# First weight copies and gate-up products ahead of finding and picking in the entry to the expert loop

## The reference, cut to what matters

```python
def _swiglu(x, w_gu, w_down):
    g, up = jnp.split(x @ w_gu, 2, axis=-1)
    return (jax.nn.silu(g) * up) @ w_down

def _moe(u, router_w, router_b, exp_w_gu, exp_w_down, shared_w_gu, shared_w_down):
    scores = jax.nn.sigmoid((u @ router_w).astype(jnp.float32))
    _, idx = lax.top_k(scores + router_b.astype(jnp.float32), TOP_K)
    ...
    routed = lax.map(lambda a: _routed_experts(a[0], a[1], a[2], exp_w_gu, exp_w_down), (u, idx, wts))
    return routed + _swiglu(u, shared_w_gu, shared_w_down)
```

## Time and profile before

| | us |
|---|---|
| median of 3 runs | 1243.19 |
| lowest and highest of them | 1238.89, 1243.43 |
| the profiled execution's own time | 1243.38 |
| its span in the trace | 1241.7 |
| from find(0) to the loop's first gate_up(1), in the trace | 582.71 to 609.02 |
| one step of the loop | 11.86 |

### The profile page before, as it was taken

How to read it: one execution, slowest core, us unless ns; L and a number is a source line. 1 busy time by engine, 2 the same in 40 slices (tenths; PEclk the granted TensorE clock), 3 DMA queues, 4 the chain that set the end, 5 groups by cost and what they waited for, 6 DMA issues and landing times.

```text
span 1241.7 us, 20074 instructions
## 1 busy us (share of the span) xinstructions
PE 1198.1 (96%) x5713; PEld 705.4 (57%) x5714; DVE 753.3 (61%) x1283; ACT 464.4 (37%) x549; POOL 289.3 (23%) x323
## 2 busy tenths in 40 slices
PE   5899999999999999998999999999999999999995
PEld 5688887777888888883434344343443443434332
DVE  4532457586562676867556566565565656767568
ACT  5562223746422413231324334333343443444301
POOL 1000000000000000003344353443444435545400
PEclk9798999999999999999999999999999999999988
DMA  9633502353485485646788889888888898999596
GB/s 342 185 125 102 170 35 102 102 183 135 158 323 202 140 279 191 220 174 242 285 334 331 313 319 342 315 322 325 312 335 299 323 338 325 418 410 412 223 422 252
DMA packets 88593, 321.56 MB, mean 259 GB/s; under 512 B 13040, under 2 KB 16344, under 8 KB 66152
## 3 DMA queue, kind: packets, MB, share of 16 engines
q1 hardware_dynamic: 69192, 279.69, 61.2%
q0 software_dynamic: 14432, 32.85, 6.9%
q10 hardware_dynamic: 4928, 8.49, 2.0%
HBM read 292.35 MB, written 48.24 MB: 274 GB/s over the span
## 4 chain that ended last, share of the span: by engine, by line
PE 89%; DVE 6%; issue 2%; ACT 2%; DMA 1%; DVEq 0%; POOL 0%; SPq 0%; POOLq 0%; ACTq 0%
PE psum L1666 33%; PE psum L1900 28%; PE psum L1910 14%; PE psum L1889 4%; PE psum L1639 2%; PE psum L1768 1%; DVE stage L1602 1%; PE psum L1699 1%; PE psum L1939 1%; DMA ring<-in_ada_w 1%; PE psum L1757 1%; PE psum L1824 1%; PE psum L1728 1%; PE psum L1960 1%; PE psum L1680 1%
## 5 line engine op out<-in xcount | busy, mean ns | idle before, releaser
L1900 PE MATMUL psum<-w_now,xT 128*64 128x512 f32 x1568 | 347.3, 595 | 0.6 <-DVE w_now L1500 0.6
L1900 PEld LDWEIGHTS psum<-w_now,xT 128*64 128x64 f32 x1568 | 108.7, 137 | 197.4 <-issue 196.2
L733 POOL COPY w_now<-stage 128x2048 f32 x79 | 149.6, 1911 | 284.6 <-PE psum L1910 239.3
L1910 PE MATMUL psum<-w_now,mask 128*64 128x512 f32 x784 | 179.1, 599 | 4.0 <-POOL w_now L733 4.0
L1006 ACT ACTIVATE w_now<-stage 128x2048 f32 x79 | 147.6, 1906 | 37.6 <-issue 35.0
L468 DVE TENSOR_TENSOR w_lo<-ring,w_hi 128x1024 fp32r<-128x1024 f32 x80 | 94.6, 1222 | 84.2 <-ACT w_hi L461 82.3
L1666 PE MATMUL psum<-uT_hi,w_hi 128*128 128x512 f32 x352 | 139.0, 395 | 1.1 <-DVE w_lo L468 1.1
L1666 PE MATMUL psum<-uT_hi,w_lo 128*128 128x512 f32 x352 | 137.0, 389 | 0.0
L1666 PE MATMUL psum<-uT_lo,w_hi 128*128 128x512 f32 x352 | 137.0, 389 | 0.0
L461 ACT ACTIVATE w_hi<-ring 128x1024 fp32r<-128x1024 f32 x80 | 82.7, 1056 | 123.5 <-PE psum L1666 60.7
L1013 ACT ACTIVATE sel<-psum 128x256 f32<-128x256 f32 x49 | 18.9, 385 | 290.5 <-PE psum L1900 290.5
(11 more groups left out here) (357 smaller groups left out, 1674.2 us busy)
## 6 DMA issues: line engine op xcount, KB each, us to landing
stage<-in_exp_w_gu SPq DMA_DIRECT2D x106, 1024.0 KB
stage<-in_exp_w_down SPq DMA_DIRECT2D x53, 1024.0 KB
ring<-in_w_in SPq DMA_DIRECT2D x56, 512.0 KB, 5.4
expert_rows<-zero_fill SPq DMA_DIRECT2D x16, 1024.0 KB, 8.7
ring<-in_ada_w SPq DMA_DIRECT2D x32, 512.0 KB, 4.8
stage<-expert_rows SPq DMA_DIRECT2D x12, 1024.0 KB, 20.8
ring<-in_ada_w SPq DMA_DIRECT2D x4, 1024.0 KB, 13.4
scale_w<-in_ada_w SPq DMA_DIRECT2D x4, 1024.0 KB, 14.7
```

Of the source, the lines that this page charges most:

```text
L733: pool.tensor_copy(w_now[:, q, 4:6], staged(turns[q] + STAGES - 1, 4, 2)).then_inc(dn_moved, 1)
L1900: mm = pe.matmul(moe_bank(GU)[at, :], xT[:, s % 2, k, at], gu_part(q, k), start=(k == 0), stop=(k == KT - 1))
L1910: mm = pe.matmul(moe_bank(Y0 + g)[at, :], hT[:, j, at], dn_part(q, j, g), start=(j == 0), stop=(j == 1))
```

## The change

Four engines could be concerned; three programs are edited (ScalarE, VectorE, TensorE). No instruction is added or removed, only the order of each engine's own work changes.

```diff
@@ ScalarE
             act.nop().then_inc(y_ready, 2)
+            act.wait_ge(tables_ready, 1)
+            move_second(0)
             rows_turned(0, 0)
-            act.wait_ge(tables_ready, 1)
             shared_gate(1)
-            move_second(0)
+            silu(0)
             rows_turned(1, 1)
-            silu(0)
             move_second(1)
@@ VectorE
             find_rows(1, 1)
+            move_first(0)
             pick_rows(2)
             shared_up(0)
             find_rows(2, 2)
             pick_rows(3)
-            move_first(0)
             find_rows(3, 3)
             pick_rows(AHEAD)
+            gated_up(0)
             shared_up(1)
-            gated_up(0)
             move_first(1)
@@ TensorE
             find(1)
             shared_products(4)
-            find(2)
-            shared_products(1)
             wait_emptied(pe, "bstart_row")
             turn_rows(0, 0, 16)
             shared_products(2)
-            find(3)
-            shared_products(4)
-            turn_rows(1, 1, 16)
             pe.wait_ge(tables_ready, 1)
             wait_emptied(pe, ("sgu", 0))
             gate_up(0, 0, pe.value_load(copies_thru[0:1, 0:1], min_val=1, max_val=TABLE))
+            find(2)
+            shared_products(2)
+            find(3)
+            shared_products(3)
+            turn_rows(1, 1, 16)
```

## The result

The changed kernel takes 1249.03 us (median of 5 runs, 1248.67 to 1251.66), the kernel before 1243.19: a ratio of 1.0067 with a 95% interval of 1.0051 to 1.0082, so 6.3 to 10.2 us slower. I had forecast 1244.8, in a range up to 1248.5, and 0.90 for no change beyond half a per cent.

A forecast was written before the change was run, and what follows sets the result against it. TensorE was taken to bound the kernel. Its 2.0 us of idle would become 1.05 + 0.65 + 0.95 + 1.1 = 3.75, gate_up(1) 1.6 later, so 1243.19 goes to 1244.8 us, range 1240.5 to 1248.5.

The forecast's parts named there:

- The bound: Whole kernel: TensorE bounds it, busy for 1198.1 of 1241.7 us, with no other engine over 61%.
- the 2.0 us as all that there was to win: TensorE's idle from 590.13 to gate_up(1) at 609.02, claimed as all the edit can win.
- gate_up(0) 5.4 us earlier than before: First gate_up on TensorE: forecast at 594.5, 6.0 us earlier, with ACT's copy of rows as its releaser.
- The gather's landing: Before turn_rows(0): gather(0) taken to land at 591.2, leaving TensorE idle 1.05 us.
- find(3) behind an idle: Before find(3) on TensorE: idle of 0.95 us, waiting for the selection in VectorE's chain.
- The loads: SyncE's queue: loads 2 and 3 issued 8.1 us later, costing nothing, with a thin margin on one half.
- Rival 2: Late loads bite: load 2 or 3 reaches the copies late and each of 8.1 us counts; 1251.5 in full, chance 0.06.
- My own sign of being wrong: Wrong if TensorE's idle from 590.1 to gate_up(1) is below 2.5 us, or gate_up(2) follows gate_up(1) by over 11.9 us.
- Rival 1: POOL's copies hold VectorE up, gated_up(0) ends late, TensorE's transposes of h wait: 1.9 us more, 1246.7, chance 0.14.
- What is hidden at no cost: Step claiming silu(0), gated_up(0), move_down(0), shared_up and shared_gate cost TensorE nothing; gated_up(0) has the thinnest cover.
- the order itself: TensorE's stretch to gate_up(1): new order makes it 1.6 us later, between 1.7 by idle and 1.5 by starts.
- one more hold-up of 1.1 and 0.9: Upper bound of +3.5 us at gate_up(1): 0.9 more for weight copies and another 1.1 hold-up in VectorE's chain.

The follow-up runs named there:

- e7: Kernel before with second half of tables behind pick_rows(2), shared_up(0) behind move_first(0), one shared product moved ahead of turn_rows(0), move_down(0) behind gather(3): ratio 0.9977.
- e2: Changed kernel with TensorE's wait for the last shared bank moved from ahead of the loop to ahead of down_rows: ratio 1.0011 to the kernel before.
- e5: Changed kernel with GpSimd's move_down(0) behind gather(3) instead of ahead of it: ratio 1.0042 to the kernel before.
- e8: Kernel before with only GpSimd's move_down(0) put behind gather(3): ratio 0.9993.
- e6: Kernel before with TensorE's order kept and only the weight copies ahead: move_first(0) before pick_rows(2), move_second(0) before rows_turned(0). Ratio 1.0024.
- e1: Kernel before with one line changed on VectorE, gated_up(0) ahead of shared_up(1): ratio 1.0060.
- e3: Changed kernel with shared_up(1) ahead of pick_rows(4) on VectorE: ratio 1.0053 to the kernel before.
- e4: Changed kernel with four more 128x512 products that nobody reads, behind turn_rows(1) on TensorE: ratio 1.0042 to the kernel before.
- e9: Kernel before with the tables split and one shared product moved as in e7, GpSimd's order unchanged: ratio 0.9999.

## Why the prediction was wrong

*Right.* The bound, and the 2.0 us as all that there was to win: e7 took them and no more. gate_up(0) 5.4 us earlier than before (forecast 6.0), with ACT's copy of the rows as its releaser, and VectorE's copies at 2.36. The gather's landing ended a wait before turn_rows(0), of 1.84 us (forecast 1.05). find(3) behind an idle, 0.71 for 0.95. The loads: issued 19.9 us behind L1527, 8.9 later than before (forecast 8.1), and nothing waited for them; gate_up(2) follows gate_up(1) by 13.24, but by 11.86 in e2, whose loads are just as late. Rival 2 is out. My own sign of being wrong, gate_up(2) more than 11.9 us behind gate_up(1), did come, but from the clock. Rival 1 named the right hold-up, and its size in the sum was right: gated_up(0) ended at 21.3 behind L1527, where I had 21.4. But what it made late was shared_up(1) and not TensorE's transposes of h, and by e5 it is 2.3 of the 8.8 us at gate_up(2).

*The step that failed* is "What is hidden at no cost", in the words "shared_up and shared_gate are wanted by nobody before the end". TensorE has a wait for the last shared bank, which shared_up(1) empties, right ahead of the loop, and it stands in the code beside the lines edited. Before, shared_up(1) ended at 603.91 (603.22 and 0.69 us), 3.6 us ahead of the end of gate_up(0), and the 3.45 us in which TensorE takes in the loop's first instructions lay under those products, with 0.15 to spare. No idle of before shows this wait, because none was left. TensorE's sequencer does: the loop's first register load starts 0.2 us behind the end of shared_up(1), in the middle of gate_up(0). From the kernel before, the timeline and the sequencer's row (columns as in e2):

```profile
603.22 0.69 DVE L1375 TENSOR_TENSOR mods<-tmp_tok,psum 128x512 f32<-128x512 f32 x1
...
L514 PEldq TENSOR_LOAD <-live_count x1: 316/316/316, 604.1 to 604.1; - x1
```

The change moved shared_up(1) behind gated_up(0), let the picking ahead of both run beside GpSimd's copies, put the last shared products 8.9 us later, and moved gate_up(0) from just above this wait to far in front of it. Both covers, the early shared_up(1) and the long products, went at once.

*The sum, as the runs give it*, to gate_up(2): 8.8 us. 2.25 is the order itself (e2, forecast 1.6). 4.16 is the later turn_rows(2), 25.34 behind L1527 against 21.18 in e2: the wait for shared_up(1) and the entry. 2.39 is the slow turn and gate-up, 15.66 from the turn to gate_up(2) against 13.27. By the timed ratio it is 6.3 to 10.2. The 5.8 between the two medians is less, and the 3.5 us by which the profiled execution after was ahead at L1527 show how such a difference can hide. I had the entry nowhere in the sum and the clock nowhere in the range: a bound that added one more hold-up of 1.1 and 0.9 was no bound. (Its upper end, 1248.5, is also 0.9 more than its terms give: 1243.19 + 3.5 + 0.9 is 1247.6.)

*Open.* What the low clock depends on, and how often it falls in executions that aren't profiled: no run here tells.

## What to carry to other kernels

When a block of long products is moved, list every wait that stood behind it on its engine, with what was late by less than the block: such waits show as no idle, and only the sequencer's rows tell where the engine stood. An engine's entry into a loop has a price of its own, here 3.45 us, which a queue of earlier work must cover. And where two engines' copies hold each other up, give them different times: here VectorE's two first copies took 2.36 us in place of 5.39 once GpSimd's came later (e8), and with the tables split as well the kernel got faster (e7), while moving the copies forward alone made it slower (e6).

## What the runs showed of the hardware

TensorE's entry into the loop, from the end of shared_up(1) to the first transpose, took 3.44 to 3.46 us in five kernels (the change, e1, e3, e4, e5) and 3.41 in e9. Its sequencer's own rows show what it is made of: three loads of a register from SBUF, of 0.31 to 0.33 us each, with register arithmetic, checks and branches between them, one behind the other, from 607.2 to 610.2. The first and the last of them in the kernel after (columns as in e2):

```profile
L514 PEldq TENSOR_LOAD <-live_count x1: 316/316/316, 607.2 to 607.2; - x1
...
L1934 PEldq SEQ_ASSERT  x1: 18/18/18, 610.2 to 610.2; - x1
```

The granted clock fell to 0.50 inside single idles of 3.89, 4.92 and 5.28 us. After idles of 3.77 us (e5) and 3.30 us (e3) it fell 1.0 and 1.5 us behind the start of the turn that ended them, and in e4, with no idle above 1.84 us in this whole entry, as gate_up(1) began. Against the same stretch at full clock it cost 1.6 to 3.0 us each time.
